# Last two expert pairs of a top-2 mixture-of-experts tail: rows brought back to the tokens through a DRAM table, or by weighted 0/1 products on TensorE

## The chip, the cores and the metric

One NeuronCore of a Trainium2 chip runs the whole program. The metric is device microseconds of one execution; lower is better.

## The reference

Two transformer-like blocks run over 256 tokens of width 1024. Everything up to the last part (attention, pooling, a short convolution, two MLPs, a state-space branch, latent attention, cross attention) is the same in both kernels. The part that matters is the end, a mixture of 32 experts with two experts per token, and a norm:

```python
w_top = jax.nn.softmax(top_v, axis=-1) * g_w          # two weights per token
combine = sum(one_hot(expert_id, 32) * w_top[..., None], axis=1)
act = jax.nn.silu(hg) * hu * combine[:, :, None]      # hg, hu: t @ w_gate[e], t @ w_up[e]
y = jnp.einsum('tef,efd->td', act, w_down)
out = rms_norm_2(h + y, norm_final)
```

The kernel doesn't compute every expert for every token. It sorts the 512 (token, choice) rows by expert, runs each expert on its own rows, and adds each token's two result rows with their weights.

## The kernel before

Five engines run hand-written instruction streams, ordered by semaphores. The experts are worked on in blocks `n` = 0 to 19 (`NB` = 20), each of two experts with 64 rows each; `ORDER[n]` says which pair block `n` holds. Sixteen blocks hold the 16 pairs of experts. Four more (`EXTRA_AFTER`) are for experts with over 64 rows. Blocks 18 and 19 are ordinary pairs, 14 and 15.

A block on TensorE (from line 1476 on) is `gate_up(n, 0)` and `gate_up(n, 1)` (the gate and up products, 16 matmuls each at L1480, in bank 0 or 1), `turn_act(n)` (two transposes, L1491) and `down(n)` (16 matmuls, L1506, into two banks of 4 to 7). Between them ScalarE takes silu (L2049), VectorE multiplies (L2948) and copies the turned activations out (`copy_acts`, L2958). `copy_y` takes the two halves of the result out of the banks, on ScalarE (L2056) and VectorE (L2966), into `y_rows`, which has two buffers. TensorE's order is `gate_up(n, 0)`, `turn_act(n - 1)`, `gate_up(n, 1)`, `down(n - 1)`, so that the steps of one block cover the waits of the other.

The weights are the large traffic: 6 MB a pair. SyncE loads them in units of 1 MB into a ring of 17 units (`ring_order`, `load_unit`, L802 and L804), in the order in which TensorE uses them; a unit is loaded again when its last user is done. Weights of blocks that have no rows aren't moved. The loads of `final_row` (512 KB, L820) come last on that queue.

GpSimd stores each block's 128 rows to the DRAM table `ytab` (`result_rows`) with an indirect DMA (L3100); rows that belong to no token are skipped. When the stores of all 20 blocks have landed (`y_stored`), `gather` issues four indirect DMAs (L3065), one for each of two token blocks and two choices, 512 KB each, from `ytab` into `y_back`. VectorE then forms `x + w1 * first + w2 * second` in `y_sum` (L2996 for 1024 columns, L3002 for twice 512), ScalarE squares and sums it (L2095) and takes the root (L2099), VectorE takes the reciprocal (L3007) and scales (L3010), and SyncE stores the four pieces of 128x512 (L826).

The tensor `y_back` lies where the sorted columns `cols_by_place` lie, from which each block's windows are copied; `choose` and `acts` share `expert_hidden`. The split weights of the earlier stages (`weights_parts`) start 64 bytes past a multiple of 512 bytes within a partition, after the 64 bytes of `half_rows`.

Of the kernel before, what the change touches and what calls it, by code (L numbers as in the profile page):

```python
# [27 lines left out]
ALU = mybir.AluOpType  # L28
# [56 lines left out]
RING = 17  # L85

# [268 lines left out]
def build_two_blocks(nc, a, out):  # L355
# [3 lines left out]
    with ExitStack() as ctx:  # L359
# [145 lines left out]
        def unit_left(engine, use, e):  # L505
# [25 lines left out]
        y_sum = results[:, 4 * D:6 * D].rearrange("p (b d) -> p b d", b=TB)  # L531
# [12 lines left out]
            "gain_in", "final_in", "back_in00", "back_in01", "back_in10", "back_in11", "gates_half", "gates_full", "y_full", "scaled_x", "x_squared", "half_mean", "root_done",  # L544
# [286 lines left out]
        def _(pe):  # L831
# [679 lines left out]
            for n in range(NB + 1):  # L1511
                if n < NB:
                    gate_up(n, 0)
                if n:
                    turn_act(n - 1)
                if n < NB:
                    gate_up(n, 1)
                if n:
                    down(n - 1)


        @block.scalar
        def _(act):
# [556 lines left out]
            for n in range(1, NB + 1):  # L2080
# [5 lines left out]
                if n >= 2:  # L2086
                    copy_y(n - 2)
            copy_y(NB - 1)
            act.activation(roots[:, 0:1], eps_col[:, 0:1], ACT.Sqrt)

            for tb in range(TB):
                for half in range(2):
                    part = slice(half * 512, (half + 1) * 512)
                    act.wait_ge(s["y_scaled"], 8 + 3 * tb + 2 + half)
                    act.activation(y_back[:, 0, tb, part], y_sum[:, tb, part], ACT.Square,  # L2095
                                   accum_out=sums[:, 2 * half + tb:2 * half + tb + 1]).then_inc(s["final_sums"], 1)
                act.wait_ge(s["half_mean"], 2 + tb)
                act.wait_ge(s["final_sums"], 2 * tb + 2)
                act.activation(roots[:, 2 + tb:3 + tb], sums[:, 2 + tb:3 + tb], ACT.Sqrt, bias=half_mean[:, tb:tb + 1],  # L2099
                               scale=1.0 / D).then_inc(s["final_root"], 1)  # L2100
# [3 lines left out]
        def _(dve):  # L2104
# [775 lines left out]

            def first_rows():

                dve.tensor_copy(row_in[0:ROWS, :], consts[0:ROWS, C_ROW:C_ROW + 1])
# [85 lines left out]
            for n in range(1, NB + 1):  # L2969
# [7 lines left out]
                if n >= 2:  # L2977
                    copy_y(n - 2)
                copy_acts(n - 1)
                for part in ((), (1, 2), (3, 4), (5,))[n] if n < 4 else ():  # L2980
                    more_blocks(part)
                if n in (4, 5):
                    (places, mixing_weights)[n - 4]()
            copy_y(NB - 1)

# [151 lines left out]
```

## Time and profile before

| | us |
|---|---|
| median of three runs | 1241.28 |
| lowest and highest of them | 1235.68, 1241.53 |
| the profiled execution | 1234.28 |
| its span, first to last instruction | 1232.5 |
| last `down` starts | 1205.74 |
| last matmul over | about 1209.4 |
| first `gather` issued | 1214.48 |
| last scaling over | 1230.03 |

The rows below are in us from the span's start. A timeline row is start, duration, engine, line, operation, output<-inputs, shapes and count; the square bracket at its end is the idle time of that engine just before and what ended it. PE is TensorE, DVE VectorE, ACT ScalarE, POOL GpSimd. A row with "x16" merges sixteen instructions, and its duration runs from the first start to the last end. A matmul's own duration holds a latency that the next one overlaps. In a row of windows the engines' busy time is followed by the granted clock of TensorE as a share of 2.4 GHz, the mean busy share of the 16 DMA engines, and GB/s.

### The profile page before, as it was taken

Reading aid. Unit: us, or ns where it says so; the run is one execution under the profiler, and the core shown is the slowest. Engines: PE = TensorE matmul, PEld = TensorE weight load, DVE = VectorE, ACT = ScalarE, POOL = GpSimd, SP = SyncE. Lnnn points to the kernel's source line nnn. Section 1 sums busy time; section 2 is a strip of 40 time slices with the busy share of each in tenths; the row PEclk is TensorE's granted clock in tenths of the full one; section 3 lists DMA queues with packets and bytes.
Section 4 is the critical chain, followed back from the end, with each engine's and each line's share of the span. In section 5 each row is a group of like instructions: output and inputs, shape, how many; then the busy total and the mean of one; then the engine's idle time right before and its main releaser. Section 6 shows DMA issues by size and latency. Waiting matters only on the chain. (4 is left out here: it accounts for less than half of the span.)

```text
span 1232.5 us, 22410 instructions
## 1 busy us (share of the span) xinstructions
PE 1179.9 (96%) x9056; PEld 1000.1 (81%) x9056; DVE 783.6 (64%) x1316; ACT 608.3 (49%) x993; POOL 100.0 (8%) x102
## 2 busy tenths in 40 slices
PE   9999999999999999999999989999999999999992
PEld 7989999999999999899999988899999833333320
DVE  6876655566755566999899889879655552221213
ACT  6665554455544554767655576665554331111101
POOL 0000100000200000000000030010100004341301
PEclk9999999999999999999999999999999999999997
DMA  9654566564456656445444384365543999999993
GB/s 303 203 172 137 189 189 198 185 196 146 162 181 195 193 182 197 137 152 173 155 137 138 109 274 139 104 205 168 186 160 124 421 360 412 417 413 414 412 404 130
DMA packets 161045, 270.28 MB, mean 219 GB/s; under 512 B 17625, under 2 KB 126142, under 8 KB 156862
## 3 DMA queue, kind: packets, MB, share of 16 engines
q1 hardware_dynamic: 149872, 260.53, 60.6%
q0 software_dynamic: 10720, 8.42, 2.3%
q8 instruction: 60, 0.98, 0.3%
q14 instruction: 27, 0.22, 0.1%
q10 hardware_dynamic: 366, 0.12, 0.0%
HBM read 287.89 MB, written 13.63 MB: 245 GB/s over the span
## 5 line engine op out<-in xcount | busy, mean ns | idle before, releaser
L2128 DVE TENSOR_TENSOR weights_parts<-ring,weights_parts 128x1024 fp32r<-128x1024 f32 (+3 forms) x312 | 363.5, 1185 | 138.4 <-ACT weights_parts L1546 138.0
L1546 ACT ACTIVATE weights_parts<-ring 128x1024 fp32r<-128x1024 f32 (+3 forms) x312 | 309.1, 1011 | 144.6 <-PE psum L885 143.9
L883 PE MATMUL psum<-xnorm_parts,weights_parts 128*128 128x256 f32 x852 | 243.4, 286 | 6.8 <-DVE arena L2531 3.2
L884 PE MATMUL psum<-xnorm_parts,weights_parts 128*128 128x256 f32 x852 | 237.5, 279 | 0.0
L885 PE MATMUL psum<-xnorm_parts,weights_parts 128*128 128x256 f32 x852 | 237.5, 279 | 0.0
L883 PE MATMUL psum<-expert_cols,weights_parts 128*128 128x256 f32 (+1 forms) x688 | 192.5, 280 | 3.5 <-DVE expert_cols L2146 2.2
L884 PE MATMUL psum<-expert_cols,weights_parts 128*128 128x256 f32 (+1 forms) x688 | 190.1, 276 | 0.0
L885 PE MATMUL psum<-expert_cols,weights_parts 128*128 128x256 f32 (+1 forms) x688 | 190.1, 276 | 0.0
L883 PE MATMUL psum<-hidden_parts,weights_parts 128*128 128x256 f32 x640 | 178.7, 279 | 3.0 <-DVE hidden_parts L2599 1.7
L884 PE MATMUL psum<-hidden_parts,weights_parts 128*128 128x256 f32 x640 | 177.1, 277 | 0.0
L885 PE MATMUL psum<-hidden_parts,weights_parts 128*128 128x256 f32 x640 | 177.1, 277 | 0.0
L883 PEld LDWEIGHTS psum<-xnorm_parts,weights_parts 128*128 128x128 f32 x852 | 160.9, 189 | 11.0 <-DVE arena L2531 4.3
L884 PEld LDWEIGHTS psum<-xnorm_parts,weights_parts 128*128 128x128 f32 x852 | 160.3, 188 | 1.1 <-issue 0.9
L885 PEld LDWEIGHTS psum<-xnorm_parts,weights_parts 128*128 128x128 f32 x852 | 160.5, 188 | 0.0
L883 PEld LDWEIGHTS psum<-expert_cols,weights_parts 128*128 128x128 f32 (+1 forms) x688 | 128.7, 187 | 5.0 <-DVE expert_cols L2146 2.3
L884 PEld LDWEIGHTS psum<-expert_cols,weights_parts 128*128 128x128 f32 (+1 forms) x688 | 128.8, 187 | 0.3
L885 PEld LDWEIGHTS psum<-expert_cols,weights_parts 128*128 128x128 f32 (+1 forms) x688 | 128.7, 187 | 0.0
L883 PEld LDWEIGHTS psum<-hidden_parts,weights_parts 128*128 128x128 f32 x640 | 120.2, 188 | 3.8 <-issue 3.8
L884 PEld LDWEIGHTS psum<-hidden_parts,weights_parts 128*128 128x128 f32 x640 | 120.4, 188 | 0.0
L885 PEld LDWEIGHTS psum<-hidden_parts,weights_parts 128*128 128x128 f32 x640 | 120.1, 188 | 0.0
L1480 PE MATMUL psum<-expert_raw,expert_rows 128*64 128x512 f32 x240 | 61.3, 595 | 0.0
L1557 ACT ACTIVATE arena<-psum 128x512 f32<-128x512 f32 (+2 forms) x64 | 32.8, 528 | 34.3 <-PE psum L885 33.2
(452 smaller groups left out, 1723.8 us busy)
## 6 DMA issues: line engine op xcount, KB each, us to landing
ring<-in_mlp_w_up SPq DMA_DIRECT2D x32, 1024.0 KB, 5.4
ring<-in_mlp_w_down SPq DMA_DIRECT2D x32, 1024.0 KB, 4.8
ring<-in_w_in SPq DMA_DIRECT2D x30, 1024.0 KB, 5.1
ring<-in_attn_w_qkv SPq DMA_DIRECT2D x12, 1024.0 KB, 6.0
expert_raw<-in_w_exp_gate SPq DMA_DIRECT2D x22, 512.0 KB
expert_raw<-in_w_exp_up SPq DMA_DIRECT2D x22, 512.0 KB
ring<-in_w_exp_down SPq DMA_DIRECT2D x9, 1024.0 KB
expert_raw<-in_w_exp_down SPq DMA_DIRECT2D x9, 1024.0 KB
```

The lines of the kernel that those rows point to most:

```text
L883: pe.matmul(out, lh, rh, start=start, stop=False, **more)
L884: pe.matmul(out, lh, rl, start=False, stop=False, **more)
L885: return pe.matmul(out, ll, rh, start=False, stop=stop, **more)
L1480: mm = pe.matmul(bank2(buf)[ROWS * e:ROWS * (e + 1)], xe[:, buf, e, k, :], gates_of(n, part, e)[:, :, k % 4 * DE:(k % 4 + 1) * DE], start= ...
L1546: ins = act.activation(high, src, ACT.Copy)
L1557: act.activation(dst, view(b) if view else bank2(b), ACT.Copy).then_inc(made[b], 1)
L2128: ins = dve.tensor_tensor(low, src, high.bitcast(F32), ALU.subtract)
```

## The change

The results of blocks 18 and 19 don't go through `ytab`. A matrix `back` of 128 rows by 256 tokens for each of the two blocks holds a token's weight where a row of the block is one of the token's two rows, and zero elsewhere; TensorE multiplies it with the block's `y_rows` and sums over both blocks in four banks.

- VectorE builds the matrix in `way_back` (12 instructions, at block step 6), TensorE turns it with four transposes (`turn_back`, after `down(6)`), VectorE copies it out (`copy_back`).
- TensorE's order at the end becomes `turn_act(18)`, `down(18)`, `gate_up(19, 0)`, `rows_back(0, 0)`, `gate_up(19, 1)`, `rows_back(0, 1)`, `turn_act(19)`, `down(19)`, `rows_back(1, 0)`, `rows_back(1, 1)`. The ring loads the weights of `down(18)` ahead of those of `gate_up(19, ...)`.
- GpSimd stores 18 blocks in place of 20 and gathers after the 18th. It waits as well until the last windows have been copied, since `y_back` lies on their source. The rows of `ytab` that no block stored are zero.
- VectorE adds the four gathered pieces onto the residual in place (`y_sum` is now `x_nat`), 1024 columns an instruction, and then the four banks, half by half. Both halves of the last result are copied out by ScalarE. Squares, roots and scaling follow as before, with the sums ordered by halves.

No tensor is added, resized or moved. The diff, cut:

```diff
+LAST = NB - 1
+TURNED_IN = 7
 def ring_order():
     uses = [("gates", 0, 0), ("gates", 0, 1)]
-    for n in range(1, NB):
+    for n in range(1, LAST):
         uses += [("gates", n, 0), ("gates", n, 1), ("down", n - 1, None)]
-    return uses + [("down", NB - 1, None)]
+    return uses + [("down", LAST - 1, None), ("gates", LAST, 0), ("gates", LAST, 1), ("down", LAST, None)]
...
-        y_sum = results[:, 4 * D:6 * D].rearrange("p (b d) -> p b d", b=TB)
+        y_sum = x_nat
+        count_row = arena_rest[:, 256:256 + ROWS]
+        sum_bank = ((0, 2), (4, 5))
...
+            def turn_back():
+                pe.wait_ge(s["back_ready"], 8)
+                for q in range(2):
+                    for tb in range(TB):
+                        mm = pe.transpose(bank(2 + TURNED_IN % 2)[:, (2 * q + tb) * P:(2 * q + tb + 1) * P],
+                                          back_nat[:, tb, q, :], ident)
+                mm.then_inc(s["back_turned"], 1)
+            def rows_back(q, half):
+                n = LAST - 1 + q
+                pe.wait_ge(s[("y_first", "y_second")[half]], n + 1)
+                for tb in range(TB):
+                    mm = pe.matmul(bank(sum_bank[half][tb]), back[:, q, tb, :], y_rows[:, n % 2, half * 512:(half + 1) * 512],
+                                   start=(q == 0), stop=(q == 1))
+                    if q == 1:
+                        mm.then_inc(s["rows_back"], 1)
...
+            turn_act(LAST - 1)
+            down(LAST - 1)
+            gate_up(LAST, 0)
+            rows_back(0, 0)
+            gate_up(LAST, 1)
+            rows_back(0, 1)
+            turn_act(LAST)
+            down(LAST)
+            rows_back(1, 0)
+            rows_back(1, 1)
...
+            def way_back():
+                for choice, w in enumerate(("w1", "w2")):
+                    ins = dve.tensor_tensor(placed[:, choice], chosen[:, choice], spread(rt(w), NE), ALU.mult)
+                link(ins)
+                link(dve.tensor_tensor(placed[:, 0], placed[:, 0], placed[:, 1], ALU.add))
+                link(dve.tensor_tensor(placed[:, 1], rt("late"), same(window_at[:, 0:NE], TB), ALU.subtract))
+                for q in range(2):
+                    for e in range(2):
+                        slot = 2 * ORDER[LAST - 1 + q] + e
+                        for tb in range(TB):
+                            dve.tensor_scalar(back_nat[:, tb, q, ROWS * e:ROWS * (e + 1)], count_row,
+                                              placed[:, 1, tb, slot:slot + 1], placed[:, 0, tb, slot:slot + 1],
+                                              ALU.is_equal, ALU.mult).then_inc(s["back_ready"], 1)
...
+            for tb in range(TB):
+                for choice, w in enumerate(("w1", "w2")):
+                    dve.wait_ge(s[f"back_in{tb}{choice}"], 16)
+                    link(dve.scalar_tensor_tensor(y_sum[:, tb, :], y_back[:, choice, tb, :], rt(w)[:, tb, :], y_sum[:, tb, :],
+                                                  ALU.mult, ALU.add))
+            for half in range(2):
+                part = slice(half * 512, (half + 1) * 512)
+                for tb in range(TB):
+                    if half and tb:
+                        dve.wait_ge(s["final_sums"], TB)
+                        dve.tensor_scalar(half_mean, sums[:, 0:TB], 1.0 / D, EPS, ALU.mult, ALU.add).then_inc(s["half_mean"], 1)
+                    dve.wait_ge(s["rows_back"], 2 * half + tb + 1)
+                    dve.tensor_tensor(y_sum[:, tb, part], bank(sum_bank[half][tb]), y_sum[:, tb, part],
+                                      ALU.add).then_inc(s["rows_added"], 1)
...
-            for n in range(NB):
+            for n in range(LAST - 1):
                 pool.wait_ge(s["y_first"], n + 1)
...
             for i in range(2):
-                pool.wait_ge(y_stored[i], 16 * ((NB + 1 - i) // 2))
+                pool.wait_ge(y_stored[i], 16 * ((LAST - i) // 2))
+            pool.wait_ge(s["window_first"], NB)
+            pool.wait_ge(s["window_second"], NB)
             gather()
```

## Rows read from the trace of the kernel before

**Rows 1.** The chain that ended last, in order of time: start, us, what.

```profile
1210.96 0.96 DMA result_rows<-squares,slot_rows
1211.92 1.80 issue
```

**Rows 2.** Windows of the block phase and of the end of its loads.

```profile
1100.00:1150.00 50.00, 50.00 (x234) 16.48 (x232) 9.72 (x18) 8.07 (x15) 19.01 (x20) 1.00 1.03 414
...
1205.00:1206.00 1.00, 0.26 (x2) 0.23 (x4) 0.60 (x2) 0.00 (x0) 0.00 (x0) 1.00 0.16 66
1206.00:1207.00 1.00, 1.00 (x6) 0.35 (x4) 0.00 (x0) 0.00 (x0) 0.90 (x1) 1.00 0.02 8
```

**Rows 3.** Timeline of the last two blocks, all engines.

```profile
1190.80 3.60 PE L1480 MATMUL psum<-ring,expert_rows 128*64 128x512 f32 x16
...
1191.01 0.69 DVE L2966 COPY squares<-psum 128x512 f32<-128x512 f32 x1 [2.40 <-PE psum L1506]
...
1192.54 0.96 POOL L3100 DMA_INDIRECT result_rows<-squares,slot_rows  x1 [9.86 <-DVE squares L2966]
...
1195.21 3.65 PE L1480 MATMUL psum<-expert_weights,expert_rows 128*64 128x512 f32 x16 [0.44 <-DMA expert_weights<-in_w_exp_up]
...
1198.91 0.38 ACT L2049 ACTIVATE cos_t<-psum 128x256 f32<-128x256 f32 x1 [9.02 <-PE psum L1480]
1199.32 0.60 DVE L2948 TENSOR_TENSOR std<-psum,cos_t 128x256 f32<-128x256 f32 x1 [4.09 <-ACT cos_t L2049]
...
1200.88 3.65 PE L1506 MATMUL psum<-expert_weights,expert_hidden 128*64 128x512 f32 x16 [2.02 <-DMA expert_weights<-in_w_exp_down]
...
1204.47 0.44 PE L1491 MATMUL psum<-consts_sb,std 128*128 128x128 f32 x2
...
1205.18 0.41 DVE L2958 COPY expert_hidden<-psum 128x256 f32<-128x256 f32 x1
...
1205.74 0.61 PE L1506 MATMUL psum<-expert_rows,expert_hidden 128*64 128x512 f32 x1 [0.84 <-DVE expert_hidden L2958]
...
1207.72 0.60 ACT L2056 ACTIVATE squares<-psum 128x512 f32<-128x512 f32 x1 [4.26 <-PE psum L1506]
...
1209.44 0.69 DVE L2966 COPY squares<-psum 128x512 f32<-128x512 f32 x1 [3.84 <-PE psum L1506]
```

**Rows 4.** Timeline of the gathers, the sums, the norm and the output.

```profile
1214.48 1.03 POOL L3065 DMA_INDIRECT results<-result_rows,place_ids  x1 [2.56 <-issue]
...
1218.43 0.99 POOL L3065 DMA_INDIRECT results<-result_rows,place_ids  x1 [0.30 <-issue]
1219.04 1.28 DVE L2996 SCALAR_TENSOR_TENSOR results<-results,rope_a,xres 128x1024 f32<-128x1024 f32 x1 [8.91 <-DMA results<-result_rows,place_ids]
...
1221.87 0.63 ACT L2095 ACTIVATE results<-results 128x512 f32<-128x512 f32 x1 [12.04 <-DVE results L3002]
1222.41 0.19 ACT L2095 ACTIVATION_READ_ACCUMULATOR results<-results 128x1 f32 x1
...
1223.97 1.28 DVE L2996 SCALAR_TENSOR_TENSOR results<-results,rope_a,xres 128x1024 f32<-128x1024 f32 x1 [1.19 <-DMA results<-result_rows,place_ids]
...
1227.56 0.30 ACT L2099 ACTIVATE rope_b<-rope_b 128x1 f32<-128x1 f32 x1
...
1228.42 0.16 DVE L3007 RECIPROCAL rope_b<-rope_b 128x1 f32<-128x1 f32 x1
1228.62 1.41 DVE L3010 SCALAR_TENSOR_TENSOR results<-results,rope_b,expert_hidden 128x512 f32<-128x512 f32 x2
```

**Rows 5.** Timeline of TensorE: two matmuls of 128 rows by 512 columns, back to back.

```profile
607.71 1.02 PE L1206 MATMUL psum<-arena 128*128 128x512 f32 x2
```

**Rows 6.** DMA issues: KB each, us from issue to landing.

```profile
expert_hidden<-in_norm_final SPq DMA_DIRECT2D x1, 512.0 KB, 20.0
...
result_rows<-zeros POOLq DMA_DIRECT2D x4, 512.0 KB, 8.9
```

**Rows 7.** L3065, the third and fourth gather alone.

```profile
DMA to landing us min/median/max: 6.7/6.8/6.8
```

More of the change, by code:

```diff
@@ L1509, in down @@
                     mm.then_inc(s["y_full"], 1)
[L1511 to L1513 removed]
+            def turn_back():
[13 more added lines that the diff above has]
+                        mm.then_inc(s["rows_back"], 1)
+            for n in range(LAST):
+                gate_up(n, 0)
                 if n:
+                    if n == TURNED_IN + 1:
+                        pe.wait_ge(s["back_copied"], 1)
                     turn_act(n - 1)
[L1516 to L1517 removed]
+                gate_up(n, 1)
                 if n:
                     down(n - 1)
+                if n == TURNED_IN:
+                    turn_back()
+            turn_act(LAST - 1)
[8 more added lines that the diff above has]
+            rows_back(1, 1)
         @block.scalar
@@ L2984, in _ @@
-            copy_y(NB - 1)
-            dve.wait_ge(s["final_in"], 16)
-            def half_mean_of(tb):
-                dve.wait_ge(s["final_sums"], 2 * tb + 1)
-                dve.tensor_scalar(half_mean[:, tb:tb + 1], sums[:, tb:tb + 1], 1.0 / D, EPS, ALU.mult,
-                                  ALU.add).then_inc(s["half_mean"], 1)
-            for tb in range(TB):
-                dve.wait_ge(s[f"back_in{tb}0"], 16)
-                dve.scalar_tensor_tensor(y_sum[:, tb, :], y_back[:, 0, tb, :], rt("w1")[:, tb, :], x_nat[:, tb, :],
-                                         ALU.mult, ALU.add).then_inc(s["y_scaled"], 1)
-                dve.wait_ge(s["y_scaled"], 8 + 3 * tb + 1)
-                dve.wait_ge(s[f"back_in{tb}1"], 16)
-                for half in range(2):
-                    part = slice(half * 512, (half + 1) * 512)
-                    dve.scalar_tensor_tensor(y_sum[:, tb, part], y_back[:, 1, tb, part], rt("w2")[:, tb, :],
-                                             y_sum[:, tb, part], ALU.mult, ALU.add).then_inc(s["y_scaled"], 1)
-                half_mean_of(tb)
+                if n in (4, 5, 6):
+                    (places, mixing_weights, way_back)[n - 4]()
@@ new lines, in _ @@
+            for tb in range(TB):
[3 more added lines that the diff above has]
+                                                  ALU.mult, ALU.add))
+            for half in range(2):
+                part = slice(half * 512, (half + 1) * 512)
+                for tb in range(TB):
+                    if half and tb:
[4 more added lines that the diff above has]
+                                      ALU.add).then_inc(s["rows_added"], 1)
```

39 lines of the change are left out of this document (25 added, 14 removed).

## The prediction

> **What bounds the kernel now.** I read the end first, because the change lies there. The chain that ended last runs, from the last `down` on, through one store, its landing, four gathers, sums, norm and output. The last `down` starts at 1205.74 [rows 3] and the span ends at 1232.5, so 26.8 us follow in which TensorE has 3.7 us of work. Of these the store of block 19 takes 2.76 us from issue at 1210.96 to landing at 1213.72 [rows 1]; the gathers are issued at 1214.48 and, the fourth, at 1218.43 [rows 4], and the last two need 6.8 us to land [rows 7].
>
> Then the blocks. In 50 us of the block phase TensorE is busy 50.00, at the full granted clock of 2.4 GHz, and the DMA engines are busy all the time too, at 414 GB/s [rows 2]. Both are full: TensorE has never waited for weights until 1195.21 (0.44 us) and 1200.88 (2.02 us) [rows 3]; the loads end about 1206 (busy share 0.16, then 0.02 [rows 2]). So work added to TensorE earlier costs its length until the wait for the last weights takes over; and what the DMA engines move before 1206 may delay weights.
>
> **TensorE up to the last down.** `turn_back` is four transposes; two take 0.44 us [rows 3], the pair after them about 0.2 more: 0.7, uncovered. `gate_up(19, 0)` starts at 1190.80 now [rows 3]; there `turn_act(18)` would start at 1191.5. VectorE's `copy_y(17)` goes from 1191.01 + 0.7 for 0.69, `copy_acts` 0.41, and `down` starts 0.15 after that copy (1205.59 to 1205.74) [rows 3]: 1192.96. This gap of 1.5 us is new, since no gate product covers the turning any more. `down(18)` takes 3.65, `gate_up(19, 0)` 3.60 [rows 3]. A `rows_back` pair is priced by two matmuls of the same shape: 1.02 for two [rows 5], where one takes 0.61 by L1506 [rows 3], so about 0.42 more for each further one. TensorE reaches `gate_up(19, 1)` at 1201.2, or 1200.8 where the steps overlap by the 0.15 seen elsewhere. Its weights now have the place of `down(18)`'s, which were there at 1200.88 [rows 3]. I take 1200.9. It ends at 1204.55; silu and the product end 1.06 after the gates (1198.86 to 1199.92) [rows 3], 1205.6, and `rows_back(0, 1)` fits into this gap (1.02). Turn 0.44, copy 0.41: 1206.5. The last `down` starts at 1206.65, 0.9 later than now; its weights have landed by then.
>
> **The matrix.** `way_back` has 12 VectorE instructions of at most 128x64; none is shown, so from below nothing, from above the 0.41 of a 128x256 copy [rows 3]: 4.9 us, I take 2.5. It stands behind `copy_acts(5)`; what queues behind it is the product of block 6, which TensorE asks for only after a `down` and a gate product, 7 us later. `copy_back` (0.69 by the nearest copy) is asked for after a gate product of 3.6. Both are hidden; uncovered they would cost TensorE 4.9 and 0.7. The copy of `count_row` lies in a stretch where VectorE is ahead of block 0 and costs nothing (at most 0.4).
>
> **The gathers.** The store of block 17 is issued at 1192.54 now, 0.84 after its copy [rows 3]; with the shift of 0.7, at 1193.24. Its landing isn't shown. From below it is the 2.76 of the store at 1210.96, when nothing else moved [rows 1]; from above the 8.9 of stores of 512 KB from GpSimd's queue, and further off the 20.0 of the 512 KB of `final_row` that stood in SyncE's queue [rows 6]. The DMA engines are full at 1193, and the queue is GpSimd's: 8.9, so 1202.1. The first gather follows 0.76 later (1213.72 to 1214.48), the fourth 3.95 after it [rows 1, 4], and lands after 6.8 [rows 7]: 1213.65. The wait for the last windows that now stands ahead of the gathers is met long before, when the gates of block 17 are done; behind it GpSimd has nothing else. VectorE adds a piece in 1.30 (1.28 and a gap) [rows 4]; four from 1206.5 would end at 1211.7, and the fourth gather makes it **X = 1214.95**. TensorE is done before: the second half of the last result is ready 3.70 after the start of `down` (1205.74 to 1209.44), copied by ScalarE in 0.60 [rows 3], and the last pair of `rows_back` ends at 1212.1. So six of its eight matmuls are hidden or nearly, and the other two end ahead of the gathers.
>
> The Trainium skill (SBUF — State Buffer, section Who interferes with whom) says that a VectorE instruction with two SBUF inputs and a GpSimd instruction that reads SBUF block each other for the whole instruction. The trace doesn't show it: the sum at 1219.04 ran while the fourth gather was issued and took 1.28, like the one at 1223.97 with GpSimd idle [rows 4]. By the rule the first sum could start 1.0 late; since X hangs on the fourth gather, the end would stay.
>
> **From X to the end.** Two adds out of the banks, 0.69 each (nearest: L2966) [rows 3], with ScalarE's two squares (0.63, and 0.19 for the sum) behind: X + 2.3. Mean 0.16, fourth add: X + 3.15. The third square and a root (0.30): X + 3.4. Reciprocal 0.16 and two scalings 1.41, twice, the second root being ready in time: X + 6.6 [rows 4]. The output takes 2.47 after the last scaling, as now (1230.03 to 1232.5). X + 9.05: the span ends at **1224.0**, 8.5 us before 1232.5, or 0.7%. The profiled execution took 1234.28, so 1225.8. It is below all three timed runs, whose median is 1241.28; taken from that, 1232.8. I give 1232, since the runs that count are such runs.
>
> **Rivals.**
>
> *The gathers aren't the last.* If they land 2 us earlier, X is 1211.75 by VectorE's four sums and the end 1220.8: a gain of 11.7. For it: the first gather lands faster than the last two, and the engines are nearly idle after 1206 [rows 2]. Against it: the four are issued in the same way as now.
>
> *Gathers and weights collide.* If the store lands after 2.76, the gathers run from 1197 to 1202, while weights still come. Their 2 MB at 414 GB/s are 5.07 us; the last weights come at 1211.0, X is 1216.1 and the end 1225.1: a gain of 7.4. For it: the DMA engines are full up to 1197 or so. Against it: the same fullness keeps the store from landing early. The Trainium skill (DMA: Bandwidth & Descriptors, section Queues, rings and completion order) says that each DMA engine takes turns, packet by packet, between the queues that have work. The 8.9 of rows 6 agrees with taking turns better than the 20.0 does.
>
> *The store stands behind the weights (slower).* Place: GpSimd's wait for block 17's store. Price: as `final_row`, 20.0 us [rows 6]: 1213.25, and with 0.76, 3.95, 6.8, 1.30 and 9.05 behind it the end is 1235.1, 2.6 us slower. It costs the whole gain from a landing 17.4 us after issue on, is below what can be measured from 11.2 on, and measurably slower from 23.6 on. Against it: the 20.0 is a place in SyncE's own queue (at 414 GB/s it is some 8 MB deep), and the store is in another.
>
> *The block phase pays.* If the new waits there cost TensorE 3 us, full as it is, 5.5 are left. Against it: the slack of 7 and 3.6 us above.
>
> *The change doesn't do all it says.* No tensor moves, so the split weights lie where they lay and the stages ahead keep their time; this part of the description is worth nothing, and I count on nothing from it.
>
> **How the numbers follow.** Forecast 0.52; gathers not last 0.14; collision 0.16; store late 0.10; block phase 0.08. A measurement of this kernel tells 0.5%, or 6.2 us, from no change. The first two cases, and most of the third, gain more: 0.75. Slower by over 0.5% needs the late store at its worst or something unseen: 0.06; between, 0.19. The range has to hold both levels at which the kernel before ran: from 1234.3 less 11.7, 1222.5, to the median less some 3 (late store up to about 14 us, or the block phase), 1238.
>
> **What would show it.** Right: L1480 of block 19 after two L1506 groups, the last `down` at 1206.7, the first gather near 1202.9, the fourth landing near 1213.7, VectorE's four sums waiting for it, and 9 us from the last sum to the end. Wrong: `down(19)` waiting for weights past 1208 (collision); the first gather after 1210 (late store); TensorE idle at `turn_back`, eleven blocks ahead of 1190.80 (block phase); TensorE's granted clock at its lower level ahead of the last matmuls, where it is 1.00 now [rows 2]; or the four adds waiting for `rows_back` and not for the gathers.

## The result, and the profile after

The kernel after took 1229.24 us (median of 20 runs, 1223.14 to 1240.02), the kernel before beside it 1236.36 us (20 runs): the medians are 7.1 us apart. The ratio of the runs is 0.9935, with a 95% interval of 0.9913 to 0.9957, which is 8.0 us less, between 5.3 and 10.8. One slow run of before, 1320.69 us, is not in that ratio. The forecast was 1232.0 and a gain of 8.5.

The profiled execution of after is the slowest of its 20 runs: 1240.02 us, with a span of 1238.0 against 1232.5 of before, and the two spans can't be set against each other as they are. The stages ahead of the blocks have the same instructions in both kernels, and they differ from run to run. What the change touches starts with the first gate product of block 0. I cut the span there, and once more at the first gate product of block 18; what follows the second cut is called the tail.

The two cuts in before, from its timeline (start, duration, engine, line, operation, output<-inputs, shapes, count):

```profile
989.12 2.37 PE L1480 MATMUL psum<-expert_raw,expert_rows 128*64 128x512 f32 x10
...
1179.97 1.46 PE L1480 MATMUL psum<-expert_raw,expert_rows 128*64 128x512 f32 x6
```

The same cuts in after, with `turn_back` (L1522) between them, and then the steps of the tail. In after the gates stand at L1486, the turning at L1497, `down` at L1512, `rows_back` at L1531, the gathers at L3128, the sums at L3055 and the adds out of the banks at L3064.

```profile
1003.88 2.37 PE L1486 MATMUL psum<-expert_raw,expert_rows 128*64 128x512 f32 x10
...
1086.64 0.66 PE L1522 MATMUL psum<-consts_sb,expert_hidden 128*128 128x128 f32 x4
...
1195.48 1.03 PE L1486 MATMUL psum<-expert_raw,expert_rows 128*64 128x512 f32 x4
...
1206.40 0.44 PE L1497 MATMUL psum<-consts_sb,std 128*128 128x128 f32 x2
...
1207.59 3.65 PE L1512 MATMUL psum<-ring,expert_hidden 128*64 128x512 f32 x16 [0.75 <-DVE expert_hidden L3021]
...
1214.68 1.98 PE L1531 MATMUL psum<-squares,expert_hidden 128*128 128x512 f32 x4
...
1216.67 3.65 PE L1486 MATMUL psum<-expert_weights,expert_rows 128*64 128x512 f32 x16
1217.07 1.04 POOL L3128 DMA_INDIRECT results<-result_rows,place_ids  x1 [8.06 <-issue]
...
1220.25 1.99 PE L1531 MATMUL psum<-squares,expert_hidden 128*128 128x512 f32 x4
...
1222.49 0.42 DVE L3021 COPY expert_hidden<-psum 128x256 f32<-128x256 f32 x1 [1.10 <-PE psum L1497]
1223.98 5.25 DVE L3055 SCALAR_TENSOR_TENSOR xres<-results,rope_a,xres 128x1024 f32<-128x1024 f32 x4 [1.07 <-DMA results<-result_rows,place_ids]
1226.56 3.70 PE L1531 MATMUL psum<-squares,expert_hidden 128*128 128x512 f32 x8
```

The tail was 52.5 us (1179.97 to 1232.5) and is 42.5 (1195.48 to 1238.0): 10.0 less. Between the cuts lie 190.85 us before and 191.60 after: 0.75 more. Together that is 9.2 us of gain behind the first cut. The other 14.8 us, by which the first cut comes later in this profile, can't be put down to the change: the same program profiled a second time (experiment *again*) reaches that cut at 995.93, and the last section shows where such differences come from.

The chain that ended last in after (start, us, what):

```profile
1208.04 0.97 DMA result_rows<-squares,slot_rows
1209.01 7.30 issue
...
1217.07 6.89 DMA results<-result_rows,place_ids
...
1223.98 1.30 DVE xres L3055
...
1227.94 1.30 DVE xres L3055
...
1229.26 0.70 DVE xres L3064
1229.99 1.96 ACT results L2136 x6
...
1232.65 1.41 DVE xres L3073 x2
...
1234.93 0.66 DVEq L361
```

In before [rows 1, 3, 4] the chain went from the last `down` through its own store and only then to the gathers. Now it starts with the store of block 17, issued 12.6 us into the tail, ahead of the last `down` (27.5 into it). TensorE is no part of it. GpSimd goes on at 1216.31, 8.3 us after the issue of that store (the row "issue" of 7.30 is this landing). The first gather takes 6.89 to land, VectorE forms the four sums back to back, and 8.8 us of adds, norm and output follow (1229.24 to 1238.0).

A reading aid for the counts in these rows: `gate_up` and `down` make eight matmul calls each and `rows_back` makes two, as the source of the kernel has it, and their rows count x16, x16 and x4. Each of these fp32 calls leaves two records; the "16 matmuls" of the section on the kernel before are records.

### The profile page after: what moved, and what is told of

It is laid out like the page before. It is cut to its first block and busy times, and to the rows that moved or that the text cites. A ratio compares the mean times of both kernels' runs of the same rounds, so it can differ in the third digit from the quotient of the medians.

```text
span 1238.0 us, 22461 instructions
## 1 busy us (share of the span) xinstructions
PE 1205.2 (97%) x9076; PEld 1019.3 (82%) x9076; DVE 788.2 (64%) x1330; ACT 608.1 (49%) x994; POOL 97.3 (8%) x100
## 5 line engine op out<-in xcount | busy, mean ns | idle before, releaser
L889 PE MATMUL psum<-xnorm_parts,weights_parts 128*128 128x256 f32 x852 | 243.5, 286 | 6.0 <-DVE arena L2573 2.2
L891 PE MATMUL psum<-xnorm_parts,weights_parts 128*128 128x256 f32 x852 | 237.8, 279 | 0.0
L889 PE MATMUL psum<-expert_cols,weights_parts 128*128 128x256 f32 (+1 forms) x688 | 195.0, 283 | 3.5 <-DVE expert_cols L2188 2.2
L890 PE MATMUL psum<-expert_cols,weights_parts 128*128 128x256 f32 (+1 forms) x688 | 192.6, 280 | 0.0
L891 PE MATMUL psum<-expert_cols,weights_parts 128*128 128x256 f32 (+1 forms) x688 | 192.6, 280 | 0.0
L889 PE MATMUL psum<-hidden_parts,weights_parts 128*128 128x256 f32 x640 | 181.6, 284 | 3.1 <-DVE hidden_parts L2641 1.7
L890 PE MATMUL psum<-hidden_parts,weights_parts 128*128 128x256 f32 x640 | 179.9, 281 | 0.0
L891 PE MATMUL psum<-hidden_parts,weights_parts 128*128 128x256 f32 x640 | 179.9, 281 | 0.0
L889 PEld LDWEIGHTS psum<-xnorm_parts,weights_parts 128*128 128x128 f32 x852 | 161.2, 189 | 10.6 <-issue 4.3
L891 PEld LDWEIGHTS psum<-xnorm_parts,weights_parts 128*128 128x128 f32 x852 | 160.4, 188 | 0.0
L889 PEld LDWEIGHTS psum<-expert_cols,weights_parts 128*128 128x128 f32 (+1 forms) x688 | 130.2, 189 | 5.0 <-DVE expert_cols L2188 2.3
L891 PEld LDWEIGHTS psum<-expert_cols,weights_parts 128*128 128x128 f32 (+1 forms) x688 | 129.5, 188 | 0.0
L889 PEld LDWEIGHTS psum<-hidden_parts,weights_parts 128*128 128x128 f32 x640 | 122.0, 191 | 3.9 <-issue 3.9
L891 PEld LDWEIGHTS psum<-hidden_parts,weights_parts 128*128 128x128 f32 x640 | 121.6, 190 | 0.0
L890 PEld LDWEIGHTS psum<-hidden_parts,weights_parts 128*128 128x128 f32 x640 | 121.2, 189 | 0.0
L1486 PE MATMUL psum<-expert_raw,expert_rows 128*64 128x512 f32 x240 | 61.3, 595 | 0.0
```

The source lines that it names most:

```text
L889: pe.matmul(out, lh, rh, start=start, stop=False, **more)
L890: pe.matmul(out, lh, rl, start=False, stop=False, **more)
L891: return pe.matmul(out, ll, rh, start=False, stop=stop, **more)
L1486: mm = pe.matmul(bank2(buf)[ROWS * e:ROWS * (e + 1)], xe[:, buf, e, k, :], gates_of(n, part, e)[:, :, k % 4 * DE:(k % 4 + 1) * DE], start= ...
```

## The experiments

**What was asked.** My theory was that the end hangs on the landing of block 17's store and on what VectorE and the DMA engines do behind it, and that TensorE's products and its new order cost next to nothing. The rivals were that the products bound the end, that gathers and weights collide, and that the place of the split weights, which the change's description speaks of, has a part in the gain. All readings "into the tail" are from the first gate product of block 18 of the same run. An empty row in the table parts the groups of kernels that ran on one chip in one go.

| kernel | us (ratio to before, interval) | tail | first gather issued, into the tail | last `down`, into the tail |
|---|---|---|---|---|
| before | 1236.36 | 52.5 | 34.5 | 25.8 |
| after | 1229.24 (0.9935, 0.9913 to 0.9957) | 42.5 | 21.6 | 27.5 |
| | | | | |
| again | 1231.28 (0.9942, 0.9917 to 0.9967) | 41.8 | 21.6 | 27.4 |
| w512 | 1254.25 (1.0128, 1.0098 to 1.0159) | 41.7 | | |
| one_pair | 1232.00 (0.9952, 0.9917 to 0.9986) | 45.8 | 25.7 | |
| old_order | 1229.34 (0.9918, 0.9888 to 0.9948) | 41.9 | 21.8 | 26.2 |
| | | | | |
| no_first | 1231.65 (one run) | 41.5 | 21.6 | 25.9 |
| early_gather | 1230.74 (one run) | 46.9 | 9.6 | 32.9 |
| gain_late | 1231.50 (0.9908, 0.9869 to 0.9947) | 43.1 | 21.1 | 27.4 |
| before512 | 1262.30 (1.0184, 1.0154 to 1.0214) | 51.2 | 34.3 | 25.5 |
| | | | | |
| gain_last | 1229.94 (0.9923, 0.9890 to 0.9956) | 41.3 | 21.1 | 27.4 |
| past32 | 1244.13 (1.0027, 1.0006 to 1.0049) | 41.9 | | |
| past128 | 1249.24 (1.0060, 1.0040 to 1.0081) | 41.8 | | |
| past256 | 1253.03 (1.0098, 1.0053 to 1.0143) | 41.5 | | |

A tail can be read to a tenth of a microsecond in one profile, but kernels with the same steps in the tail gave 41.5 to 42.5 (after, again, w512, past32, past128, past256), and 51.2 and 52.5 (before512, before). The spread lies in the landings: in five of the six the first gather is there 27.5 to 28.5 us into the tail, and the tail is that plus 14.0 to 14.1 (in w512 the third gather comes last); the last two gathers took 6.7 to 6.8 us to land in before and 5.3 to 5.5 in before512. A single time can't show a microsecond; a tail shows two.

**again.** The kernel after, unchanged, on the chip of the next three.

> The changed kernel once more, as the base of the comparisons of this call. What is compared is the tail, from the first gate product of block 18 to the end of the span: 52.5 us in the profile of the kernel before, 42.5 in that of the changed one, which loses 0.75 to the transposes ahead of it. My theory (the end hangs on the landing of block 17's store, then the first gather, four sums on VectorE of 1.3 us each, adds, norm and output): tail 42.5 within 0.7, the time 9.3 us or 0.75% below the kernel before, ratio 0.990 to 0.995. A rival (TensorE's new order and its products set the end) expects the same here.

It took 1231.28 us, 0.9942 of before. Its cut at block 0 is here:

```profile
995.93 1.08 PE L1486 MATMUL psum<-expert_raw,expert_rows 128*64 128x512 f32 x4
```

That is 8.0 us ahead of the first profile of after, with the same instructions. So the longer span of that profile says nothing against the change.

**old_order.** Both pairs go by products, but TensorE, the ring and the copies of the results keep the order of before. The order of TensorE, cut out of the diff:

```diff
-            turn_act(LAST - 1)
-            down(LAST - 1)
             gate_up(LAST, 0)
-            rows_back(0, 0)
+            turn_act(LAST - 1)
             gate_up(LAST, 1)
-            rows_back(0, 1)
+            down(LAST - 1)
             turn_act(LAST)
+            rows_back(0, 0)
             down(LAST)
+            rows_back(0, 1)
```

> Both pairs come back by products, but TensorE and the weights' ring keep the order of the kernel before (gates of block 19 ahead of the down of block 18), and the first products stand around the last down. My theory: the gathers, and with them the sums, come when they came: tail 42.5 within 0.7; the last down starts about 1.7 us earlier, and three pairs of products stand behind it instead of two, so TensorE ends about where it ended (34.8 us into the tail). The rival (the new order and its gap of 1.2 us at the turning of block 18 cost the end): tail 41.0 or less.

Measured: a tail of 41.9, within 0.2 of *again*, and 1229.34 us. Its sums and its products:

```profile
1216.50 5.25 DVE L3051 SCALAR_TENSOR_TENSOR xres<-results,rope_a,xres 128x1024 f32<-128x1024 f32 x4 [2.49 <-DMA results<-result_rows,place_ids]
...
1218.56 5.42 PE L1531 MATMUL psum<-squares,expert_hidden 128*128 128x512 f32 x12
...
1224.01 0.69 DVE L3060 TENSOR_TENSOR xres<-psum,xres 128x512 f32<-128x512 f32 x1
```

Here the last products end at 1223.98 and the last add follows at 1224.01: the products are last, though only just, since the sums are over at 1221.75. In after the sums are last. The two orders differ in what is late and not in the end: the tails are 0.2 apart, so the new order of the last two blocks brings no gain that these runs can show.

**one_pair.** Block 18 goes back through the table, and the gathers wait for its store; only block 19 goes by products. The diff, cut:

```diff
             gate_up(LAST, 0)
-            rows_back(0, 0)
             gate_up(LAST, 1)
-            rows_back(0, 1)
...
-            for n in range(LAST - 1):
+            for n in range(LAST):
```

> Only block 19 comes back by products; block 18 is stored, and the gathers follow its store. My theory: the store of block 18 is issued 17.3 us into the tail (block 17's: 12.6), and everything behind it follows: with the 8.2 us landing of block 17's store and 6.9 for the first gather the tail is 47.2; as the weights are nearly all in by then the store may land in 4 to 5, and the tail is 43.5 to 44. So 43.5 to 47.2, always longer than 42.5. The rival (TensorE's products set the end): two pairs of products fewer, 1.7 us of them on the path, so a tail of 40.8.

```profile
1187.19 1.03 PE L1486 MATMUL psum<-expert_raw,expert_rows 128*64 128x512 f32 x4
...
1212.90 1.04 POOL L3126 DMA_INDIRECT results<-result_rows,place_ids  x1 [7.40 <-DMA result_rows<-squares,slot_rows]
...
1222.60 1.28 DVE L3053 SCALAR_TENSOR_TENSOR xres<-results,rope_a,xres 128x1024 f32<-128x1024 f32 x1 [0.39 <-DMA results<-result_rows,place_ids]
```

The gathers are issued 25.7 into the tail, 4.1 later than in after, and the tail is 45.8, 3.3 to 4.1 longer. VectorE waits for the gathers, up to the last sum (0.39 at 1222.60). The end goes with the gathers, nearly one for one. Of the 10.0 us by which the tail is shorter, block 19 alone thus brings 6.7 (52.5 to 45.8), and block 18 the rest. The time (1232.0) is too near that of *again* to show it.

**no_first.** The kernel after without its products of block 18, whose rows are missing from the output. The diff, cut:

```diff
             gate_up(LAST, 0)
-            rows_back(0, 0)
             gate_up(LAST, 1)
-            rows_back(0, 1)
```

> The kernel after without the products of block 18 (four calls, two of them between gate_up(19, 0) and gate_up(19, 1), two between gate_up(19, 1) and turn_act(19)); the rows of block 18 are left out of the output. Theory (the end hangs on block 17's store, the first gather, VectorE's four sums): TensorE gets to the last down about 0.6 to 2.5 us earlier, but the gathers are issued 21.6 us into the tail as before, give or take 0.3, and the tail stays at 41.7 to 42.6 us. Rival (the products on TensorE set the end): the tail is shorter by the 1.7 to 3.8 us that the left-out products take, 40.5 us or less.

```profile
1188.12 1.03 PE L1486 MATMUL psum<-expert_raw,expert_rows 128*64 128x512 f32 x4
...
1208.30 3.65 PE L1486 MATMUL psum<-expert_weights,expert_rows 128*64 128x512 f32 x16 [0.98 <-DMA expert_weights<-in_w_exp_up]
...
1209.76 1.03 POOL L3126 DMA_INDIRECT results<-result_rows,place_ids  x1 [8.12 <-issue]
...
1215.59 5.25 DVE L3053 SCALAR_TENSOR_TENSOR xres<-results,rope_a,xres 128x1024 f32<-128x1024 f32 x4 [1.62 <-DMA results<-result_rows,place_ids]
```

The last `down` starts 25.9 into the tail and not 27.4, the gathers stay at 21.6, VectorE waits 1.62 for the first of them, and the tail is 41.5. That is 0.2 below what the theory gave, and a full microsecond above what the rival gave. Four fewer calls on TensorE bring nothing that can be told from the spread of tails above: the first gather lands 27.5 into the tail (1215.57), and 14.05 us follow, as in after. The row at 1208.30 also gives a number that after hides: the last weights are there 20.2 us into the tail (1208.30 less 1188.12).

**early_gather.** Block 17's results aren't stored and are missing from the output, and the gathers wait only for block 16's store. The diff, cut (the waits for the buffers of `y_rows` are shortened to match):

```diff
-            for n in range(LAST - 1):
+            for n in range(LAST - 2):
...
-                pool.wait_ge(y_stored[i], 16 * ((LAST - i) // 2))
+                pool.wait_ge(y_stored[i], 16 * ((LAST - 1 - i) // 2))
```

> The kernel after, but block 17's results are not stored and the gathers wait only for block 16's store: the rows of block 17 are left out of the output. Theory (the gathers' issue sets the sums): the gathers are issued some 7 us earlier, about 14.5 us into the tail; the first lands by about 22, and the four sums (5.25 us) take the gaps of VectorE or stand behind copy_acts(19): X is 28 to 33 us into the tail, where TensorE's last products (about 34.8) become the last, and the tail is 40.0 to 41.5 us, 0.5 to 2 less than with block 17's store. Rival (gathers and weights collide): the last weights come up to 5 us late, the last down starts at 30 us or later into the tail instead of 27.4, and the tail is 44 us or more. Rival (the gathers don't matter): the tail stays at 41.7 to 42.6.

The tail got longer, 46.9 us; my theory had it shorter, and the collision had it right. The timeline:

```profile
1181.91 1.03 PE L1486 MATMUL psum<-expert_raw,expert_rows 128*64 128x512 f32 x4
...
1206.81 5.35 PE L1486 MATMUL psum<-expert_weights,expert_rows 128*64 128x512 f32 x16 [3.71 <-DMA expert_weights<-in_w_exp_up]
```

The landing of the four gathers, from the view of their line:

```profile
DMA to landing us min/median/max: 8.6/11.2/13.0
```

Two windows (start:end, length, busy time of PE, PEld, DVE, ACT and POOL, then granted clock, DMA share, GB/s):

```profile
1200.00:1207.00 7.00, 3.29 (x12) 1.04 (x10) 0.00 (x0) 0.00 (x0) 0.00 (x0) 1.00 0.92 379
1207.00:1211.00 4.00, 4.00 (x14) 1.26 (x13) 0.00 (x0) 0.00 (x0) 0.00 (x0) 0.64 0.40 165
```

The gathers are issued 9.6 into the tail. I had said 14.5, since I took block 16's store for one that comes 7 us before block 17's, and it comes a whole block before. They now run beside the last weights: they need 8.6 to 13.0 us to land, and the weights of `gate_up(19, 1)` are there 24.9 into the tail (1206.81 less 1181.91), 4.7 later than in *no_first*. That is close to the price that the prediction put on a collision (5.07, from 2 MB at 414 GB/s). A second cost had no price there, only a mention among the signs: TensorE stood for 3.71 us, its granted clock then averages 0.64 over the 4 us shown (0.50, its level of 1.2 GHz, from 1209 to 1211), and the gate products took 5.35 us where they take 3.65. The prediction's collision ended with a tail of 44.4 us (1225.1 less 1180.67), 2.5 short of the 46.9. The prediction cited the Trainium skill (DMA: Bandwidth & Descriptors, section Queues, rings and completion order), by which a DMA engine takes turns between its queues; this run agrees, since both the gathers and the weights came later.

So these gathers gain nothing from coming 12 us earlier. In after they start 1.4 us after the last weights have come (21.6 against the 20.2 of *no_first*), and of the loads only `final_row` is still under way.

**gain_late, gain_last.** In after, the load of `final_row` (L826) is issued 9.6 us into the tail:

```profile
1205.11 1.04 SPq L826 DMA_DIRECT2D expert_hidden<-in_norm_final  x1
```

The views of the lines L826 and, below it, L3128 (the four gathers) give the landings:

```profile
DMA to landing us min/median/max: 18.7/18.7/18.7
...
DMA to landing us min/median/max: 6.6/6.7/6.9
```

So `final_row` is there at 1223.8, just ahead of the first gather (1223.96). Seven profiles have this load and the gathers in this order, and the later the one lands after its issue, the slower is the other: 17.5 us and 5.6 (w512), 17.6 and 5.8 (no_first), 17.7 and 6.0 (past128), 17.9 and 6.1 (again and past32), 18.5 and 6.7 (past256), 18.7 and 6.9 (after). The 6.9 of after, from which the theories below reckon, is the slowest of them. Two kernels move the load: one to behind the first gather's landing, one to behind the fourth's.

```diff
             o = out.rearrange("a (b p) d -> p (a b) d", p=P)
+            sp.wait_ge(s["back_in00"], 16)      # gain_late;  "back_in11" in gain_last
             sp.dma_start(final_row, a["norm_final_2"]...
```

> The kernel after, with the load of final_row (512 KB) issued only when the first gather has landed. Theory (the first gather stands behind that load in one of the DMA engines): the first gather lands 5.0 to 6.0 us after its issue instead of 6.9, VectorE's first sum no longer waits for it, the tail is 0.7 to 1.2 us shorter (41.0 to 41.8), and the time 0.1% below that of the kernel after, too little to be told from it. Rival (the gather takes 6.9 us by its own many small pieces): landing and tail as they are, or up to 2 us longer if final_row now lands after the scalings want it (some 9 us after the first gather).

The landing of the four gathers in gain_late, and its sums in the timeline:

```profile
DMA to landing us min/median/max: 5.1/5.3/7.9
```

```profile
1213.50 3.92 DVE L3056 SCALAR_TENSOR_TENSOR xres<-results,rope_a,xres 128x1024 f32<-128x1024 f32 x3
...
1219.34 1.28 DVE L3056 SCALAR_TENSOR_TENSOR xres<-results,rope_a,xres 128x1024 f32<-128x1024 f32 x1 [1.92 <-DMA results<-result_rows,place_ids]
```

The first gather does land after 5.1 us, and three sums run without a wait; but the fourth gather, issued beside the 512 KB, now takes 7.9, the fourth sum waits 1.92 for it, and the tail is 43.1 where the theory gave 41.0 to 41.8. This time the gather issued beside the load is the slow one.

> The kernel after, with the load of final_row issued only when the fourth gather has landed. Theory (gathers and final_row share the DMA engines: with final_row first, the first gather took 6.9 us; with it in the middle, the fourth took 7.9): with all four gathers undisturbed the first lands about 5.1 us after issue, the fourth 6 to 6.8 after, about 31.6 into the tail, final_row about 3 later, ahead of the scalings at 37; the fourth sum ends at 32.0 to 33.0, the tail is 40.8 to 41.9 us, at most 1 less than the kernel after, a time within 0.2% of it. Rival (the gathers set each other's pace): the fourth lands 7.9 after its issue again, the tail is 42.5 to 43.3.

The same of gain_last, with the last products and the last add:

```profile
DMA to landing us min/median/max: 5.1/5.8/5.9
```

```profile
1216.03 5.24 DVE L3056 SCALAR_TENSOR_TENSOR xres<-results,rope_a,xres 128x1024 f32<-128x1024 f32 x4
...
1219.76 3.70 PE L1532 MATMUL psum<-squares,expert_hidden 128*128 128x512 f32 x8
...
1223.49 0.69 DVE L3065 TENSOR_TENSOR xres<-psum,xres 128x512 f32<-128x512 f32 x1
```

With `final_row` behind all four, they land in 5.1 to 5.9 us and the sums start right behind `copy_acts(19)`. The tail is 41.3, within the theory's 40.8 to 41.9, and the products end (1223.46) just as the last add wants them (1223.49). Sums and products are level now, so the next microsecond would have to come from both. Against the 41.5 to 42.5 of the kernels that leave the load where it was, 41.3 is at most 1.2 us less and no gain that these profiles can show, and the time, 0.9923 of before, can't be told from that of after.

**w512, before512.** In both kernels the split weights start 64 bytes past a multiple of 512, behind the 64 bytes of `half_rows`. Here `half_rows` is moved behind them, so that they start at the multiple; nothing else moves. Once in the kernel after (w512), once in the kernel before (before512).

```diff
-        half_rows = sb("half_rows", [P, 2, 2 * MORE], I32)
         with nc.sbuf_tensor("expert_weights", [P, 2 * UNITS * UNIT], F32) as w_plain:
             pass
         w_parts = sb("weights_parts", [P, 2 * UNITS * UNIT], F32R)
+        half_rows = sb("half_rows", [P, 2, 2 * MORE], I32)
```

> The changed kernel with the split weights at a multiple of 512 bytes, by moving the 64 bytes of half_rows behind them; nothing else. My theory: the tail does not read them; tail 42.5, and if the place means nothing the time is that of the changed kernel within 0.3%. The rival (the place of the split weights matters, as the description has it): the stages ahead of the experts, which multiply by them some 2,500 times, get longer, and the time rises by over 0.5%, with the matmul pitch in the MLPs (113 ns in the profile of the kernel before, 118 in the profile of the changed one) as the place where it shows.

> The kernel before, with the small tensor ahead of the split weights moved behind them, so that the weights start at a multiple of 512 bytes instead of 64 past one; nothing else moves and no instruction changes. Theory (the place of the weights sets the pace of TensorE's products with split weights in the stages ahead of the blocks, in either kernel alike, so it is no part of what this change brings): 1.2 to 2.2% slower than the kernel before, some 15 to 27 us, all of it ahead of the first gate product of block 0. Rival (the place matters only with the new products or in the kernel after): within 0.4% of the kernel before.

Each is 20 to 23 us slower than its own kernel: w512 1254.25 against 1231.28 of *again* in the same go (1.9%), before512 1262.30 against 1241.90 of the runs of before beside it (1.6% by the medians, ratio 1.0184). The tails stay within their spread (41.7, and 51.2 against 52.5). The loss lies ahead of the first cut, which w512 reaches here:

```profile
1019.91 1.08 PE L1486 MATMUL psum<-expert_raw,expert_rows 128*64 128x512 f32 x4
```

against 995.93 in *again*, 24.0 us later. TensorE's groups by line show where; first *again*, then w512 (busy us, mean ns of one):

```profile
L890 PE MATMUL psum<-xnorm_parts,weights_parts 128*128 128x256 f32 x852 | 237.3, 278 | 0.0
...
L891 PEld LDWEIGHTS psum<-xnorm_parts,weights_parts 128*128 128x128 f32 x852 | 160.4, 188 | 0.0
```

```profile
L890 PE MATMUL psum<-xnorm_parts,weights_parts 128*128 128x256 f32 x852 | 240.9, 283 | 0.0
...
L891 PEld LDWEIGHTS psum<-xnorm_parts,weights_parts 128*128 128x128 f32 x852 | 163.2, 192 | 0.0
```

Each weight load takes 192 ns where it took 188, each matmul 283 where it took 278. The place is worth about 2% in either kernel alike. Since the change moves no tensor, it is no part of what the change brings. The pair w512 and before512 also gives the change's own gain once more, with both at the slow place: the tail goes from 51.2 to 41.7.

**past32, past128, past256.** Is it any start off the multiple that helps? Unused bytes ahead of the split weights of after: 64 for past128, 192 for past256, and for past32 32 of them in the place of `half_rows`, which goes behind the weights. The edit of past256:

```diff
         half_rows = sb("half_rows", [P, 2, 2 * MORE], I32)
+        gap = sb("gap", [P, 48])
```

> The kernel after, with the small tensor ahead of the split weights moved behind them and 32 unused bytes in its place, so that they start 32 past a multiple of 512 bytes. If any start off the multiple does: 1225 to 1238 us. If 64 bytes are the least that helps: 1246 to 1258 us.

> The kernel after, with 64 unused bytes ahead of the split weights, so that they start 128 past a multiple of 512 bytes (all behind them moves by 64). If only a start at the multiple itself is slow: within 0.4% of the kernel after, 1225 to 1238 us. If what counts is the place within 128 bytes: 1246 to 1258 us.

> The kernel after, with 192 unused bytes ahead of the split weights, so that they start 256 past a multiple of 512 bytes instead of 64 (all that stands behind them moves by 192 as well). If only a start at the multiple itself is slow: within 0.4% of the kernel after, 1225 to 1238 us. If what counts is the place within 256 bytes: 1.2 to 2.2% slower than the kernel after, 1246 to 1258 us.

The starts at 128 and 256 came out as the second answer had it, the start at 32 between the two. With *gain_last* in the same go as the kernel at 64 (1229.94): 32 past the multiple costs 1.2% (1244.13), 128 costs 1.6% (1249.24), 256 costs 1.9% (1253.03), as much as the multiple itself did in its own go. The tails are all within 41.5 to 41.9. In these three all that lies behind the weights moves too, by 32, 64 and 192 bytes, so they aren't as clean as w512. The five places together would roughly fit a pace that goes by the start within 128 bytes and is best in the middle. That isn't shown: starts at 96 or 192 weren't tried, and 128 is some 4 to 5 us better than 0 and 256, which such a pace leaves unexplained.

## Why the prediction was right, point by point

**The sum.** Set on the first gate product of block 18 (1179.97 plus the 0.7 of `turn_back`), the prediction had a tail of 43.3 us, from 52.5, and 0.7 paid in the block phase: a gain of 8.5. The profile has 42.5 and 0.75: 9.2; the pair before512 and w512 has 51.2, 41.7 and the same 0.75: 8.8. The runs have 8.0 by their ratio, between 5.3 and 10.8. Three things in this agreement are luck: the terms below err in both directions, two profiles of one tail differ by up to a microsecond, and the 1232 was reckoned from a median of three runs (1241.28) that lies 4.9 above that of the 20.

**The way.** As predicted, the first gather moved ahead of the last `down`, the end hangs on block 17's store and the gathers behind it, and TensorE is off the chain. *one_pair* shows it from one side (gathers 4.1 later, tail 3.3 to 4.1 longer), *no_first* from the other (1.6 us of TensorE's work gone ahead of the last `down`, tail the same).

**turn_back and the matrix.** 0.66 for the four transposes, 0.75 in the block phase, where 0.7 stood. The 12 instructions on VectorE took 2.8 us (1069.25 to 1072.03), with 2.5 forecast between 0 and 4.9, and were hidden.

**The gap ahead of `down(18)`.** Forecast 1.5 from the turning to `down`; it is 1.2 (1206.40 to 1207.59). The first copy on VectorE starts 0.12 behind the turning, and the second starts 0.1 before the first is over.

**The store and the gathers.** Landing 8.9 after issue, from the 512 KB stores of the zeros [rows 6]: measured 8.3. First gather at 22.2 into the tail: 21.6. This was the term with the widest bounds, 2.76 to 20.0, and the row of the same queue beside other loads was the right one to take: the DMA engines were busy 0.67 to 1.04 while the zeros went out (729 to 741 in before), and 1.05 where block 17's store was issued.

**The step that failed: the size of `rows_back`.** I priced a pair at 1.02 us, by two rows of the same shape [rows 5]. A pair takes 1.98, and its row counts four matmuls. The two matmuls in [rows 5] are thus one call in the program, and the kernel bears it out: its L1206 makes four calls and has eight records. A product of plain fp32 leaves two records here. The rows on record could have told it, since `gate_up` makes eight calls and its row counts x16 [rows 3]. The Trainium skill (FP8 and Floating Point Precision, section TensorE Precision Notes) says that true fp32 takes four passes through the array; by an estimate from it, 4 times 512 columns, one a cycle at 2.4 GHz, a call is 0.85 us. The trace agrees: two calls took 1.98 (1214.68) and four took 3.70 (1226.56), so a further call costs 0.86. So `rows_back(0, 0)` held up `gate_up(19, 1)` by 1.0, `rows_back(0, 1)` didn't fit into the gap of 1.06 behind the gates, and the last `down` came 27.5 into the tail and not 26.0. It cost nothing that can be told (*no_first*), as the gathers were last. Of the first pair about half is hidden in any case: without it (*no_first*), TensorE waits for the last weights up to 20.2 into the tail, and with it `gate_up(19, 1)` starts at 21.2. The prediction had these weights at 20.2 too (1200.9).

**The other step that failed: which gather sets the sums.** I let the fourth gather set the last sum, X = 1214.95, 34.3 into the tail. The chain goes through the first: it lands 28.5 into the tail, and four sums of 1.30 behind it make X 33.8. The fourth had landed by then, 6.6 us after an issue at 25.6, so at 32.2, just ahead of its sum (32.5). The two ways are within half a microsecond of each other, which is why X came out nearly right: that is luck. Which gather sets the sums changes with so little: in *one_pair* the last sum does wait for the fourth. What lay behind X took 8.8, where 9.05 stood.

**The rivals.** The gathers not last: not so in after, where VectorE still waits 1.07 for the first one; in *gain_last* it no longer waits. The collision: it didn't take place, because the store lands after the last weights; *early_gather* shows that its price for the late weights was about right (4.7 for 5.07), and that the forecast had left out what TensorE's wait then costs in clock. The late store: didn't take place. The block phase paying 3 us: 0.75. That part of the description is worth nothing: right for the change, by w512 and before512, though the place itself is worth more than the whole change.

**The rule about VectorE and GpSimd.** In after no sum stands beside the issue of a gather, so the rule that the prediction cited (the Trainium skill, SBUF — State Buffer, section Who interferes with whom) wasn't needed. In *one_pair* one does:

```profile
1216.86 0.99 POOL L3126 DMA_INDIRECT results<-result_rows,place_ids  x1 [0.30 <-issue]
...
1217.38 1.28 DVE L3053 SCALAR_TENSOR_TENSOR xres<-results,rope_a,xres 128x1024 f32<-128x1024 f32 x1 [2.84 <-DMA results<-result_rows,place_ids]
```

The sum and the issue overlap by 0.47 us, and neither is longer than elsewhere. In before512 the same pair overlaps (1247.13 and 1247.66) and takes 0.99 and 1.29. So three traces, with that of [rows 4], show no blocking between a sum and the issue of a gather.

## What to carry to other kernels

When a store to memory and a gather from it stand at the end, work out what is the last block whose result has to go that way, and bring the later ones back by another engine that has time left. Earlier is not always better: here gathers that met the last weight loads (9.6 into the tail) were worse than gathers behind them (21.6). A small load that nobody waits for yet can go behind such gathers: it did no harm there, and the first gather landed in 5.1 us where it took 5.6 to 6.9 behind the load, though the gain in time is too small to be shown. Where one group of a profile prices another, count the calls in the source against the records in the row, before its duration is halved.

## What the runs showed of the hardware

The place of a tensor within SBUF sets the pace of TensorE's products with it. With nothing else changed in its instructions, the kernel took 1254 us with the split weights at a multiple of 512 bytes (beside 1231 at 64 in the same go), and in another go 1244 at 32 past it, 1230 at 64, 1249 at 128 and 1253 at 256. In the two groups shown above, the weight loads took 192 ns at 0 and at 256, and 188 at 32, 64 and 128; the matmuls took 283 at 0 and 256, 281 at 32 and 128, and 278 to 279 at 64. Which accesses, if any, hinder each other isn't shown by any of these runs and stays open.

Runs at 64 spread more (1223 to 1240 in the 20 of after, 1225 to 1237 in the 10 of gain_last) than those at the multiple (1252.9 to 1255.2 in the five of w512) or at 256 (1252.7 to 1254.2 in six). The spread lies in the stages ahead of the blocks: the cut at block 0 comes at 995.93 in *again* and at 1003.88 in after, and the tails differ by 0.8 us only. The traces show where. In the three lines of products with split weights (L889 to L891, in before L883 to L885, some 6,800 steps from the start of one matmul to that of the next that are shorter than 150 ns), a step at 64 takes 113 to 114 ns or 117 ns and more, mostly 118. The longer kind makes up 30% in before, 49% in *again* and 74% in after, and the means are 114.7, 115.6 and 116.7 ns. The 1.1 ns between *again* and after, times 6,800, is 7.5 of the 8.0 us between their cuts; the 2.0 between before and after make 13.6 of the 14.8. At the multiple 99% of the steps are of the longer kind, most of them 120 (w512). What decides between the two in a run isn't shown.
